# Fewer candidate sums in the product-key search of a two-block transformer kernel

## The reference

```python
s1, i1 = lax.top_k(s[:, :, 0], PEER_TOPK)
s2, i2 = lax.top_k(s[:, :, 1], PEER_TOPK)
cand = (s1[..., :, None] + s2[..., None, :]).reshape(..., PEER_TOPK * PEER_TOPK)
cidx = (i1[..., :, None] * PEER_NKEYS + i2[..., None, :]).reshape(...)
top, pos = lax.top_k(cand, PEER_TOPK)
idx = jnp.take_along_axis(cidx, pos, axis=-1)
g = jax.nn.softmax(top, axis=-1)
a = jax.nn.gelu(jnp.einsum('tpkd,td->tpk', u[idx], t))
return jnp.einsum('tpk,tpkd->td', g * a, v[idx])
```

## Time and profile before

| | |
|---|---|
| median of 3 runs | 2997.11 us (2995.46 to 3005.19) |
| the profiled execution: span from first to last instruction | 3102.8 us (no time of its own beside the span is given for it) |
| PE, DVE, ACT, POOL busy | 2428.4, 1928.1, 979.3, 1162.5 us |
| mean granted TensorE clock | 0.871 of full speed |
| HBM | 798.93 MB read, 258 GB/s over the span |

### The profile page before, as it was taken

How to read it: one execution, slowest core, us unless ns; L and a number is a source line. 1 busy time by engine, 2 the same in 40 slices (tenths; PEclk the granted TensorE clock), 3 DMA queues, 4 the chain that set the end, 5 groups by cost and what they waited for, 6 DMA issues and landing times.

```text
span 3102.8 us, 43837 instructions
## 1 busy us (share of the span) xinstructions
PE 2428.4 (78%) x16608; PEld 1757.3 (57%) x16608; DVE 1928.1 (62%) x4058; ACT 979.3 (32%) x1694; POOL 1162.5 (37%) x1028
## 2 busy tenths in 40 slices
PE   7898896897045555566674998957999999999998
PEld 5676775545010011111273787722777899996998
DVE  3221766488955576666698786754444676665665
ACT  4443655311000000000222433413333545455544
POOL 0000000066767777767746675666554000000000
PEclk8997998998567877778786999976999999997999
DMA  6222111289889999999998999998899445551454
GB/s 274 99 112 78 56 42 42 101 317 361 308 342 342 374 324 370 357 358 352 352 345 291 363 408 408 409 377 291 333 407 387 142 138 188 186 188 55 153 186 144
DMA packets 218946, 803.92 MB, mean 259 GB/s; under 512 B 24433, under 2 KB 27761, under 8 KB 214769
## 3 DMA queue, kind: packets, MB, share of 16 engines
q0 software_dynamic: 147456, 536.94, 46.2%
q1 hardware_dynamic: 71280, 264.19, 23.7%
HBM read 798.93 MB, written 2.10 MB: 258 GB/s over the span
## 4 chain that ended last, share of the span: by engine, by line
PE 35%; DVE 18%; issue 10%; DMA 8%; POOL 6%; another core or an unknown queue 3%; ACT 1%; DVEq 0%; SPq 0%; POOLq 0%; ACTq 0%
PE ps L1817 9%; PE ps L1819 8%; PE ps L1818 8%; DVE pe_ring L2522 7%; PE ps L1757 6%; DMA pe_ring<-in_v,pe_vidx 5%; POOL pe_ring L1706 2%; DVE la_w_lo L2570 2%; POOL pe_ring L1700 2%; DMA pe_ring<-in_u,pe_idx 1%; PE ps L1896 1%; PE ps L1922 1%; PE ps L1905 1%; POOL pe_more L1706 1%
## 5 line engine op out<-in xcount | busy, mean ns | idle before, releaser
L1757 PE MATMUL ps<-pe_ring,pe_spot 128*32 128x512 f32 x1596 | 426.8, 771 | 213.6 <-DMA pe_ring<-in_v,pe_vidx 145.6
L1700 POOL DMA_INDIRECT pe_ring<-in_u,pe_idx x424 | 502.0, 1184 | 230.5 <-issue 122.8
L2522 DVE CUSTOM_DVE_ANT_0 pe_ring<-pe_ring,pe_htok 128x1024 f32<-128x1024 f32 x424 | 505.7, 1224 | 121.3 <-DMA pe_ring<-in_u,pe_idx 90.6
L1817 PE MATMUL ps<-la_h_hi,la_w_hi 128*128 128x256 f32 x1856 | 536.8, 289 | 34.0 <-DVE la_w_lo L2570 22.3
L1819 PE MATMUL ps<-la_h_hi,la_w_lo 128*128 128x256 f32 x1856 | 528.0, 284 | 1.4 <-issue 1.1
L1818 PE MATMUL ps<-la_h_lo,la_w_hi 128*128 128x256 f32 x1856 | 527.0, 284 | 0.9 <-issue 0.9
L1706 POOL DMA_INDIRECT pe_ring<-in_v,pe_vidx x399 | 439.9, 1103 | 222.3 <-issue 112.3
L2570 DVE TENSOR_TENSOR la_w_lo<-la_w_raw,la_w_hi 128x1024 fp32r<-128x1024 f32 (+1 forms) x368 | 440.2, 1197 | 74.1 <-ACT la_w_hi L2182 58.0
L2182 ACT ACTIVATE la_w_hi<-la_w_raw 128x1024 fp32r<-128x1024 f32 (+1 forms) x368 | 380.0, 1035 | 312.9 <-DMA la_w_raw<-in_down 86.5
L1817 PEld LDWEIGHTS ps<-la_h_hi,la_w_hi 128*128 128x128 f32 x1856 | 353.6, 191 | 71.4 <-DVE la_w_lo L2570 34.3
L1818 PEld LDWEIGHTS ps<-la_h_lo,la_w_hi 128*128 128x128 f32 x1856 | 353.3, 190 | 3.3 <-issue 2.8
(11 more groups left out here) (366 smaller groups left out, 3934.2 us busy)
## 6 DMA issues: line engine op xcount, KB each, us to landing
la_w_raw<-in_gate SPq DMA_DIRECT2D x88, 512.0 KB
la_w_raw<-in_up SPq DMA_DIRECT2D x88, 512.0 KB
la_w_raw<-in_down SPq DMA_DIRECT2D x64, 448.0 KB
la_w_raw<-in_a_in SPq DMA_DIRECT2D x40, 512.0 KB
wring<-in_w_in SPq DMA_DIRECT2D x32, 512.0 KB, 4.3
la_w_raw<-in_down SPq DMA_DIRECT2D x32, 512.0 KB
xT<-in_w_mod SPq DMA_DIRECT2D x8, 1024.0 KB, 4.8
hT<-in_w_mod SPq DMA_DIRECT2D x8, 1024.0 KB, 4.8
```

The lines of the kernel that those rows point to most:

```text
L1700: pool.indirect_dma_start(row(n), None, io["u"], bass.IndirectOffsetOnAxis(idx[:, t, j:j + 1], 0)).then_inc(land[GATHERS[n][0]], 16)
L1757: return pe.matmul(ps[PER * grp:PER * grp + PER, half, :], spot[:, j // TOKENS % 2, grp, lo:lo + PER], row(n)[:, half * 512:(half + 1) * 5 ...
L1817: pe.matmul(slot(n), parts_hi[:, n % SPLIT, i, :], hi[:, k, :], start=first, stop=False)
L2522: dve.tensor_tensor_reduce(row(n), row(n), htok[:, t, :], 1.0, 0.0, ALU.mult, ALU.add, dots[:, t % 2, j:j + 1]).then_inc(dot_done, 1)
```

## The change

With both sides sorted downwards, the sum of row i and column j (from 0) has at least (i+1)(j+1)-1 sums that are no smaller. The change writes 80 sums of a head in place of 256: all 16 columns of row 0, columns 0 to 7 of rows 1 to 7, and column 0 of rows 8 to 15. That takes three instructions in place of one. The search then runs over 80 elements a head. The place is split by 8 in place of 16, and five more small instructions turn row and column of the 80 into those of the 256. For row numbers one too large the comparison uses the numbers 1 to 16, so `pe_iota16` has 17 columns.

```diff
-    iota16 = sb("pe_iota16", [P, TOPK], on=local)
+    iota16 = sb("pe_iota16", [P, TOPK + 1], on=local)
-    cand = within("la_w_hi", "pe_cand", 3 * T, [P, PAIR, TOPK, TOPK])
+    STAIR = 8
+    CAND = TOPK + 7 * STAIR + 8
+    cand = within("la_w_hi", "pe_cand", 3 * T, [P, PAIR, CAND])
+    place_t, place_e, place_d = [within("la_w_hi", f"pe_place_{x}", 3 * T + PAIR * CAND + n * PAIR * TOPK, [P, PAIR, TOPK]) for n, x in enumerate("ted")]
             def best_pairs(n):
-                shape = [P, n, TOPK, TOPK]
-                link(dve.tensor_tensor(cand[:, 0:n, :, :], top[:, 0, 0:n, :].unsqueeze(3).broadcast_to(shape),
-                                       top[:, 1, 0:n, :].unsqueeze(2).broadcast_to(shape), ALU.add))
-                sums = [cand[:, i, :, :].rearrange("p a b -> p (a b)") for i in range(n)]
+                dve.tensor_tensor(cand[:, 0:n, 0:TOPK], top[:, 0, 0:n, 0:1].broadcast_to([P, n, TOPK]), top[:, 1, 0:n, :], ALU.add)
+                dve.tensor_tensor(cand[:, 0:n, TOPK:CAND - 8].rearrange("p t (i j) -> p t i j", j=STAIR),
+                                  top[:, 0, 0:n, 1:8].unsqueeze(3).broadcast_to([P, n, 7, STAIR]),
+                                  top[:, 1, 0:n, 0:STAIR].unsqueeze(2).broadcast_to([P, n, 7, STAIR]), ALU.add)
+                link(dve.tensor_tensor(cand[:, 0:n, CAND - 8:CAND], top[:, 0, 0:n, 8:TOPK], top[:, 1, 0:n, 0:1].broadcast_to([P, n, 8]), ALU.add))
+                sums = [cand[:, i, :] for i in range(n)]
             def experts(t, u, heads):
-                dve.tensor_scalar(place[:, 0, 0:n, :], pos[:, 0:n, :], 4, None, ALU.logical_shift_right)
-                link(dve.tensor_scalar(place[:, 1, 0:n, :], pos[:, 0:n, :], TOPK - 1, None, ALU.bitwise_and))
+                dve.tensor_scalar(place[:, 0, 0:n, :], pos[:, 0:n, :], 3, None, ALU.logical_shift_right)
+                link(dve.tensor_scalar(place[:, 1, 0:n, :], pos[:, 0:n, :], STAIR - 1, None, ALU.bitwise_and))
                 link(dve.tensor_copy(placef[:, :, 0:n, :], place[:, :, 0:n, :]))
+                row_at, col_at = placef[:, 0, 0:n, :], placef[:, 1, 0:n, :]
+                dve.tensor_scalar(place_e[:, 0:n, :], row_at, 1.0, float(STAIR), ALU.is_equal, ALU.mult)
+                link(dve.scalar_tensor_tensor(place_t[:, 0:n, :], row_at, CAND / STAIR - 1.0, col_at, ALU.is_equal, ALU.mult))
+                dve.tensor_tensor(place_d[:, 0:n, :], place_e[:, 0:n, :], place_t[:, 0:n, :], ALU.subtract)
+                link(dve.scalar_tensor_tensor(row_at, row_at, 1.0, place_t[:, 0:n, :], ALU.max, ALU.add))
+                link(dve.tensor_tensor(col_at, col_at, place_d[:, 0:n, :], ALU.add))
-                                             iota16[:, :].unsqueeze(1).broadcast_to([P, n * TOPK, TOPK]), ALU.is_equal)
+                                             iota16[:, 1 - side:1 - side + TOPK].unsqueeze(1).broadcast_to([P, n * TOPK, TOPK]), ALU.is_equal)
```

More of the change, by code:

```diff
@@ L2485, in best_pairs @@
                         link(last)
-                dve.tensor_tensor(soft[:, 0:n, :], best[:, 0:n, :], best[:, 0:n, 0:1].broadcast_to(shape[:3]), ALU.subtract).then_inc(soft_arg, 1)
+                dve.tensor_tensor(soft[:, 0:n, :], best[:, 0:n, :], best[:, 0:n, 0:1].broadcast_to([P, n, TOPK]), ALU.subtract).then_inc(soft_arg, 1)
             def experts(t, u, heads):
@@ L2919, in constants @@
     c["go"] = go.reshape(P, -1)
-    c["iota16"] = np.broadcast_to(np.arange(TOPK, dtype=np.float32), (P, TOPK)).copy()
+    c["iota16"] = np.broadcast_to(np.arange(TOPK + 1, dtype=np.float32), (P, TOPK + 1)).copy()
     return c
```

## The result

The changed kernel took 2964.9 us (median of 4 runs, 2962.53 to 2988.63), the kernel before beside it 3001.2 (2995.46 to 3008.02): a ratio of 0.989 (0.985 to 0.993). I had forecast 2992.6, with 2977 as the lowest. Faster it is, by more than my range held. Run again beside 31 runs of the kernel before, it had a ratio of 0.993 (0.990 to 0.996), 21 us. Some 20 to 25 us is what I take the change to be worth; I had forecast 4.5.

The account below looks back on a forecast made before the run. DVE was taken to bind the first stage, the stream of gathers the second, DMA and PE to share the third. Savings of 0.25 + 3 x 1.42 = 4.5 us off the median 2997.1 gave 2992.6 us, range 2977 to 3003.

Parts of the forecast that it names:

- The other 12 units: Units of choose behind tile 0's stage: 17.0 us of DVE saved, priced at nothing because the stream of gathers covers them.
- rival C: New two-tensor instructions on DVE beside POOL: each held up 1.21 us, about 24 us slower, 3021 us; chance 0.10.
- The unit's price: One choose for a pair of heads on DVE: 1.42 us saved of some 16.85.
- The search: MAX8, FIND_INDEX8 and MATCH_REPLACE8 on DVE over 176 fewer elements each: 1.87 us saved for a pair of heads.
- the sums: Three addition instructions on DVE in place of one: 0.46 us against 0.80, saving 0.34 us for a pair.
- the decoding: Five added 32-element instructions on DVE, three with a link: 0.79 us more, bounds 0.40 and 1.05.
- Tile 0: Units chosen between tile 0's dots, where DVE binds: 4.5 us saved, all ahead of the gather at 777.17.
- The sign by which I argued against A: First dot after a tile 2 choose: DVE idled 1.97 us for its row, so a shorter choose would wait longer.
- A: DVE's index and dots at tiles 1 and 2: later units count too, up to 17.0 us more, 2975.6 us; chance 0.30.
- B: Gathers, third stage or PE's first sums: the 4.5 us are given back, nothing is left, 2997 us; chance 0.20.
- D: Search on DVE: a fixed price under 256 elements leaves only decoding, 1.4 us more; chance 0.02.

Follow-up runs that it names:

- a_plus12: The changed kernel with twelve MAX8 of 128 elements added behind the pair search of each pair in tiles 1 to 3; ratio 0.990 to the kernel before.
- before_again: The kernel before, unchanged, run and profiled a second time; ratio 1.005 to the kernel before.
- no_decode: The changed kernel without its five decoding instructions, so it gathers other experts, but as many; ratio 0.989 to the kernel before.
- a_match1: The changed kernel with 32 comparisons with a constant in place of the two comparisons of two tensors; ratio 0.994 to the kernel before.
- a_long: The changed kernel with six MAX8 of 128 elements added behind each pair's search, one in a single head's; ratio 0.992 to the kernel before.
- b_tail3: The kernel before with three MAX8 of 128 elements added at each unit's end, ahead of the dots, in tiles 1 to 3; ratio 0.996 to the kernel before.
- b_scalar: The kernel before with 32 additions of 16 elements and one number a partition in place of the long two-tensor addition; ratio 1.010 to the kernel before.
- a_plus3: The changed kernel with three MAX8 of 128 elements added behind the pair search of each pair in tiles 1 to 3; ratio 0.991 to the kernel before.

## Why the prediction was wrong

**The step that failed** is "The other 12 units save 12 x 1.42 = 17.0 us of DVE. I cost these at nothing: their cover is the stream of gathers." The cover is real for length: 2.5 us more in each of these units costs 3 us in all (`a_plus12`). The traces show it at work in tile 1's stage, behind choose(1,3), `before_again` first, then the changed kernel (timeline of DVE):

```profile
1041.80 1.23 DVE L2522 CUSTOM_DVE_ANT_0 pe_ring<-pe_ring,pe_htok 128x1024 f32<-128x1024 f32 x1
```

```profile
1032.50 1.23 DVE L2533 CUSTOM_DVE_ANT_0 pe_ring<-pe_ring,pe_htok 128x1024 f32<-128x1024 f32 x1 [2.21 <-DMA pe_ring<-in_u,pe_idx]
```

Where a unit ends sooner, DVE waits 2.21 us for the row to land; in the kernel before it went on at once. What I didn't see is that the stream's own pace hangs on DVE. I had the row for it, 1.99 against 0.94 us, and used it only for rival C, as a danger for the new small instructions. It was a price that the gathers paid to the dots and the other long two-tensor instructions, 37 to 50 us in these two stages, and it could fall as well as rise. It fell to 22. This is 20.6 us of the 24.6: 554.3 us in the mean of three traces before (552.3, 561.8, 548.8), 533.7 after (534.5, 534.3, 532.3).

**The unit's price** was right within 0.2 us: 1.20 us of 1.42. The search 1.83 us (653.17 to 657.78 in `before_again`, 653.12 to 655.90 here; 1.87 forecast), the sums 0.23 (0.34), the decoding -0.87 (-0.79). That it was 0.87 for three linked and two unlinked instructions bears out 0.21 and 0.08 us against the Trainium skill (VectorE: DVE Perf Modes, "The DRAIN you can't avoid"), which has a link cost nothing.

**Tile 0** was right in direction. From the first gather to gather 156 the kernels with the change in tile 0 and nothing added there (`no_decode` and `a_match1` aside) took 262.5 to 271.3 us, 266.8 in the mean of seven, those without it 266.0 to 273.2, 268.9 in the mean of six: 2 us where I had 4.5, with a scatter larger than that.

**The sign by which I argued against A** came from the disturbed profile. DVE idled 1.97 us before the first dot behind a unit of tile 2's stage there, and I expected more of it after the change; in the changed kernel the dot at 1290.96 follows pe_g at once, and in `before_again` that at 1308.83 does. The waiting for rows that I read from it is in tile 1's stage, as shown above. The 7.01 us of the earlier trace rows, the evidence for A, were in it too. POOL waits for no index from gather 156 to 568 in any of the 19 undisturbed traces. A's sum (2975.6) came nearest, by luck, for its mechanism is refuted: had the length of the units come through, `a_long` would have lost the gain again, and it didn't.

**Rival C** had the row and the wrong price: its five decoding instructions cost 5 us of gathers at most (`no_decode`), none with over 0.24 us before it. **Rivals B and D** fell with the time and with the groups of the search.

**Open:** why the old units put the dots into the late phase half of the time and the changed ones never did, in which state each starts, what holds the gathers of tile 2's stage beyond the phase, and why `b_tail3` and `b_scalar` are slow elsewhere. That the change came out on the good side is luck as far as these runs show: nothing in it was aimed at the phase. A gather's row lands 6.7 us (u) after its issue in `before_again`, so a hold shifts the dots five gathers on, against gathers that have meanwhile moved; I have not followed that loop. No version here beats the changed kernel by more than the intervals: `a_plus3`, `a_plus12` and `no_decode` overlap with it.

## What to carry to other kernels

Work that is covered can still set the pace of its cover, where the two engines hold each other up: look for the longest form of the covering instruction (1.99 us beside 0.94), count its holds, and give them a price in both directions. Here a change that gained some 2 us in tile 0, where I had priced it, freed 20 us of holds behind it. Such a price depends on where the instructions of the two engines fall against each other, so a small edit can be worth several times its own length, of either sign, and a sum of durations won't show it. Before resting on one profile that is 3% longer than the runs, take another.

## What was not expected of the hardware

- A gather's instruction on POOL that starts while DVE runs an instruction on two SBUF tensors ends 0.94 us after that instruction, less some 0.04; one that starts before it isn't held (1290.52, 0.93 us, with the dot at 1290.96 beginning inside it), and the DVE instruction isn't longer (1.23 us). The Trainium skill (SBUF — State Buffer, "Who interferes with whom") has the two contend, and the one that issues second wait. The traces agree where the gather is second. Where the dot is second they don't: it neither waits for the gather's end nor takes longer, so POOL alone pays.
- Dots that wait for rows fall into step with the gathers: in the changed kernel 93 of 110 that had waited began 0.1 to 0.3 us behind a gather's start, where they cost the next one some 0.05 us; in `before_again` 68 of 106.
- One execution of the kernel before took 3102.8 us, with stalls of up to 8.90 us inside DVE's units; in the 19 other traces no idling inside a unit was over 0.5 us.
